# A list scheduler with other costs and finer booking of the weight splits, and local scores that take the two row halves in turn

## What is computed

```python
def first_block(x, p, ...):
    h = rmsnorm(x, norm_mix_g[i]); z = h @ w_in[i]              # 1024 x 5888
    y_a = mixer_a(qa, ka, va, ...) @ w_out_a[i]                 # 8 heads of 128 over 2 key heads
    y_b = mixer_b(qb, kb, vb, rel_bias) @ w_out_b[i]            # 3 dilations x 4 heads of 64, local bands
    x = x + (gate_a * y_a + gate_b * y_b) @ w_out[i]
    x = x + jnp.square(jax.nn.relu(rmsnorm(x, g) @ w_ff1[i])) @ w_ff2[i]
    x = x + jax.nn.sigmoid(rmsnorm(x, g) @ w_ple_gate[i]) * (p[i] @ w_ple[i])

def second_block(x, mem, ...):
    x = x + 0.5 * swiglu(rms_norm(x, ...), ...)
    x = x + hybrid_mixer(...)      # retention, and differential attention: 4 heads, two maps of 64 each
    x = x + memory_attention(...)
    x = x + 0.5 * swiglu(rms_norm(x, ...), ...)
```

## Time and profile before

| | us |
|---|---|
| median of 3 runs | 2070.78 (2067.91 to 2071.4) |
| the profiled execution | 2071.25 |
| its span, first to last instruction | 2069.5 |
| granted TensorE clock, mean | 0.992 |
| TensorE busy | 2037.4 (98%) |
| DVE, ACT, POOL busy | 1122.7, 889.7, 346.8 |

### The profile page before, as it was taken

The page is one execution under the profiler, slowest core; times in us unless marked ns, Lnnn a source line. Parts: engine busy times, 40 slices in busy tenths (PEclk is TensorE's granted clock), DMA queues, the critical chain, the costliest instruction groups (busy, mean ns, idle before and its releaser), DMA issues.

```text
span 2069.5 us, 25244 instructions
## 1 busy us (share of the span) xinstructions
PE 2037.4 (98%) x9854; PEld 1696.8 (82%) x9854; DVE 1122.7 (54%) x1960; ACT 889.7 (43%) x1750; POOL 346.8 (17%) x343
## 2 busy tenths in 40 slices
PE   8999999999999999999999999999999999999997
PEld 6888778888888888878888888788898888888886
DVE  5566775445544344565443435787775664443434
ACT  5344554345433233553332325676655443332324
POOL 3214341032000000342110101232211021110102
PEclk9999999999999999999999999999999999999999
DMA  5121111243333332233232323223242032333222
GB/s 195 62 62 62 51 47 54 86 152 102 104 99 96 98 98 89 86 105 102 93 101 92 102 84 110 77 81 96 86 154 87 29 117 92 101 93 102 92 92 72
DMA packets 61636, 191.54 MB, mean 93 GB/s; under 512 B 6792, under 2 KB 14472, under 8 KB 61516
## 3 DMA queue, kind: packets, MB, share of 16 engines
q1 hardware_dynamic: 61516, 189.93, 28.8%
HBM read 187.69 MB, written 2.21 MB: 92 GB/s over the span
## 4 chain that ended last, share of the span: by engine, by line
PE 92%; DVE 4%; ACT 1%; DMA 1%; issue 0%; SPq 0%; DVEq 0%; ACTq 0%
PE bank L292 91%; PE bank L297 1%; DVE wl L469 0%; DVE tmp L181 0%; DVE work L190 0%; SPq L169 0%; ACT tmp L178 0%; DMA raw<-d_wts 0%; DMA d_tab<-tab_sb 0%; ACT wh L467 0%; ACT rsq L178 0%; DVE x_sb L181 0%; DVE tmp L184 0%; DVE work L181 0%; DVE pd L184 0%
## 5 line engine op out<-in xcount | busy, mean ns | idle before, releaser
L467 ACT ACTIVATE wh<-raw 128x512 fp32r<-128x512 f32 (+1 forms) x700 | 403.3, 609 | 896.9 <-PE bank L292 892.6
L292 PE MATMUL bank<-h_h,wh 128*128 128x512 f32 x1536 | 612.2, 399 | 7.4 <-ACT wh L467 6.4
L292 PE MATMUL bank<-h_l,wh 128*128 128x512 f32 x1536 | 602.9, 393 | 1.0 <-DVE h_l L184 1.0
L292 PE MATMUL bank<-h_h,wl 128*128 128x512 f32 x1536 | 602.4, 392 | 0.0
L469 DVE TENSOR_TENSOR wl<-raw,wh 128x512 fp32r<-128x512 f32 (+1 forms) x630 | 420.6, 693 | 57.1 <-ACT wh L467 35.1
L292 PEld LDWEIGHTS bank<-h_h,wh 128*128 128x128 f32 x1536 | 291.0, 189 | 71.8 <-ACT wh L467 6.4
L292 PEld LDWEIGHTS bank<-h_l,wh 128*128 128x128 f32 x1536 | 291.3, 190 | 63.3 <-DVE h_l L184 3.1
L292 PEld LDWEIGHTS bank<-h_h,wl 128*128 128x128 f32 x1536 | 290.8, 189 | 61.6 <-DVE wl L469 0.3
L469 POOL TENSOR_TENSOR wl<-raw,wh 128x256 fp32r<-128x256 f32 x138 | 109.0, 816 | 363.9 <-ACT wh L467 363.9
L202 POOL TENSOR_TENSOR tmp<-tmp,rstd 128x512 f32<-128x512 f32 x44 | 63.7, 1450 | 469.4 <-ACT tmp L178 469.4
L181 DVE TENSOR_TENSOR tmp<-bank,rstd 128x512 f32<-128x512 f32 x98 | 70.5, 722 | 126.7 <-PE bank L292 126.2
(11 more groups left out here) (476 smaller groups left out, 3352.3 us busy)
## 6 DMA issues: line engine op xcount, KB each, us to landing
raw<-d_wts SPq DMA_DIRECT2D x314, 512.0 KB, 3.5
raw<-d_wts SPq DMA_DIRECT2D x24, 384.0 KB, 3.0
x_sb<-d_xT SPq DMA_DIRECT2D x16, 256.0 KB, 5.2
raw<-d_wts SPq DMA_DIRECT2D x24, 128.0 KB, 2.0
d_yT<-x_sb SPq DMA_DIRECT2D x4, 384.0 KB, 3.0
tab<-d_ali SPq DMA_DIRECT2D x4, 256.0 KB, 4.1
tab<-d_dec SPq DMA_DIRECT2D x4, 256.0 KB, 3.7
mraw<-d_memT SPq DMA_DIRECT2D x8, 128.0 KB, 2.5
```

What stands on the lines that cost most here:

```text
L292: bank.done = pe.add(lambda e: e.matmul(out, lhsT, rhs, start=first, stop=True, skip_group_check=True), n, w, waits)
L467: p.th = [Op(act, lambda e, c=c: e.activation(H[:, c], raw[:, c], FN.Copy), [p.load]) for c in (slice(o, min(o + 512, width)) for o in ran ...
```

## The change

It has two parts that work together. The costs of the scheduler are replaced by others, and the parts of a weight split are booked one by one: after a panel's first two steps 0.61 us each on ACT, after the following two (DVE) or four (POOL) steps 0.69 or 0.8 us each on the engine that makes `wl`. Which engine that is, is now settled two panels ahead (`lows`), not when the panel is taken. Where `place_panels` puts the parts is not changed. And `scores_b` no longer loops over e outside: it takes two banks a piece and issues each matmul for rows 0 to 63 and then for rows 64 to 127.

```diff
     def a_act(out, in_, func, *waits, **kw):
-        cost = 0.1 + 0.00082 * size(in_) + 0.06 * ("bias" in kw) + 0.08 * ("accum_out" in kw)
+        cost = 0.19 + 0.00085 * size(in_) + 0.06 * ("bias" in kw) + 0.19 * ("accum_out" in kw)
...
     def v_tt(out, a, b, op, *waits):
-        return dve.add(lambda e: e.tensor_tensor(out, a, b, op), 0.065 + 0.00105 * size(a), waits)
+        return dve.add(lambda e: e.tensor_tensor(out, a, b, op), 0.14 + 0.00108 * size(a), waits)
...
     def p_mul(out, a, s, *waits):
-        return pool.add(lambda e: e.tensor_scalar(out, a, s, 1.0, ALU.mult, ALU.mult), 0.07 + 0.0012 * size(a), waits)
+        return pool.add(lambda e: e.tensor_scalar(out, a, s, 1.0, ALU.mult, ALU.mult), 0.17 + 0.0016 * size(a), waits)
...
     def b_mm(bank, out, lhsT, rhs, *waits):
         first, w = opened(bank)
-        n = 0.0025 + size(rhs) / 2400
-        n = max(n, 0.055) if lhsT.dtype == F32R else max(4 * n, 0.108)
+        load, n = 0.111 if size(lhsT) == 128 else 0.06, size(rhs) / 2400
+        if lhsT.dtype != F32R:
+            n = max(4 * n + 0.01, 0.112)
+        elif lhsT.shape[0] == 64 and size(lhsT) == 128:
+            n = 0.045 + 0.0002 * size(rhs)
+        else:
+            n = max(n + 0.013, load)
...
     def take(s):
...
-        behind = max(dve.t, pe.t) + 1.2 > max(pool.t, pe.t) + 2.4
-        p.low = low = pool if (behind if i > 3 else i > 0) else dve
+        p.low = low = lows.pop(i) if i in lows else pool if i > 0 else dve
...
     def ran(p):
 
         p.steps.append(marks())
-        if len(p.steps) == 3:
-            parts_here(panels[p.i - 1].done.fin if p.i else 0.0)
+        n, i = len(p.steps) - 2, p.i + 2
+        if n == 0:
+            behind = max(dve.t, pe.t) + 1.39 > max(pool.t, pe.t) + 3.2
+            lows[i] = pool if (behind if i > 3 else i > 0) else dve
+        if n < 2:
+            act.t = max(act.t, panels[p.i - 1].done.fin + 0.13 if p.i else 0.0) + 0.61
+            th_fin[i, n] = act.t
+        elif i in lows or panels[-1].i >= i:
+            low = lows[i] if i in lows else panels[i].low
+            if low is dve and n < 4:
+                dve.t = max(dve.t, th_fin[i, n - 2] + 0.13) + 0.69
+            elif low is pool and n < 6:
+                pool.t = max(pool.t, th_fin[i, (n - 2) // 2] + 0.13) + 0.8
...
     def scores_b(pr, work):
...
-            def scores(b, out, g, lq, rk):
-                q, k = qk[pr][g]
-                b_mm(b, out, q.h[hp, lq], k.h[hp, rk], q.rdy[0], k.rdy[0])
-                b_mm(b, out, q.l[hp, lq], k.h[hp, rk], q.rdy[1])
-                q.free = k.free = [b_mm(b, out, q.h[hp, lq], k.l[hp, rk], k.rdy[1])]
...
+        def scores(bs, outs, g, lq, rk):
+            q, k = qk[pr][g]
+            for x, y, tq, tk in ((q.h, k.h, q.rdy[0], k.rdy[0]), (q.l, k.h, q.rdy[1], None), (q.h, k.l, None, k.rdy[1])):
+                for b, out, hp in zip(bs, outs, heads):
+                    q.free = k.free = [b_mm(b, out, x[hp, lq], y[hp, rk], tq, tk)]
```

More of the change, by code:

```diff
@@ L448, in parts_here @@
         low = (dve if not first_parts else pool) if len(panels) < 3 else panels[-1].low
-        act.t = max(act.t, after) + 1.04
-        low.t = max(low.t, act.t - 0.5) + (2.4 if low is pool else 1.2)
+        act.t = max(act.t, after) + 1.26
+        low.t = max(low.t, act.t - 0.6) + (3.0 if low is pool else 1.39)
     def take(s):
@@ L1001, in scores_b @@
         last = []
+        heads = slice(0, 64), slice(64, 128)
+        was = []
         for e in range(2):
[L1003 removed]
             if p_free[e] is None:
                 yield lambda: p_free[e] is not None
[L1006 to L1014 removed]
@@ new lines, in scores_b @@
+            was.append(p_free[e])
+            p_free[e] = None
+        views = [views_b(e) for e in range(2)]
+        bias0 = [bias_t[0][:, hd * 256:hd * 256 + 256] for hd in (2 * pr, 2 * pr + 1)]
+        def scores(bs, outs, g, lq, rk):
[3 more added lines that the diff above has]
+                    q.free = k.free = [b_mm(b, out, x[hp, lq], y[hp, rk], tq, tk)]
@@ new lines, in exps, with biased @@
+        def exps(e, g, parts):
+            for s, blk, tk in parts:
+                tk = a_act(s, s, FN.Exp, tk, bias=nm[:, e, g, blk:blk + 1], accum_out=ss[:, e, g, blk:blk + 1])
+            last.append(tk)
+        def biased(e, b, g, blks):
+            (g0, g12), w = views[e], was[e]
+            if blks == (1, 2):
+                s = b.ap[:, :].rearrange("p (b k) -> p b k", b=2)
+                t1 = v_tt(g0[:, 1:3, :], s, bias0[e].unsqueeze(1).to_broadcast([128, 2, 256]), ALU.add, b.done, t_toe, w)
+                b.free = [t1]
+                t2 = v_red(nm[:, e, 0, 1:3], g0[:, 1:3, :], ALU.max, t1, negate=True)
+                exps(e, 0, [(g0[:, 1, :], 1, t2), (g0[:, 2, :], 2, t2)])
+            elif blks == (0, 3):
+                p0, p3 = g0[:, 0, 64:256], g0[:, 3, 0:192]
+                t1 = v_tt(p0, b.ap[:, 0:192], bias0[e][:, 64:256], ALU.add, b.done, t_toe, w)
+                t2 = v_tt(p3, b.ap[:, 256:448], bias0[e][:, 0:192], ALU.add, b.done, t_toe, w)
+                b.free = [t2]
+                t3 = v_red(nm[:, e, 0, 0:1], p0, ALU.max, t1, negate=True)
+                t4 = v_red(nm[:, e, 0, 3:4], p3, ALU.max, t2, negate=True)
+                exps(e, 0, [(p0, 0, t3), (p3, 3, t4)])
+            else:
+                bt = bias_t[g][:, (2 * pr + e) * 128:(2 * pr + e) * 128 + 128]
+                s = b.ap[:, :].rearrange("p (c k) -> p c k", c=4)
+                t1 = v_tt(g12[g], s, bt.unsqueeze(1).to_broadcast([128, 4, 128]), ALU.add, b.done, t_toe, w)
+                b.free = [t1]
+                t2 = v_red(nm[:, e, g, :], g12[g], ALU.max, t1, negate=True)
+                exps(e, g, [(g12[g][:, c, :], c, t2) for c in range(4)])
@@ new lines, in scores_b @@
+        for g, blks in ((0, (1, 2)), (0, (0, 3)), (1, None), (2, None)):
+            if not have(*qk[pr][g])():
+                yield have(*qk[pr][g])
+            yield [t.rdy for t in qk[pr][g]]
+            bs = []
+            for e in range(2):
+                bs.append((yield from bank_of(JOB)))
+            act_table(EXP)
+            if g == 0:
+                for n, blk in enumerate(blks):
+                    lo, hi = max(0, 128 * blk - 64), min(S, 128 * blk + 192)
+                    outs = [b.ap[:, 256 * n:256 * n + hi - lo] for b in bs]
+                    scores(bs, outs, 0, slice(128 * blk, 128 * blk + 128), slice(lo, hi))
+            else:
+                for c in range(4):
+                    cs = slice(128 * c, 128 * c + 128)
+                    scores(bs, [b.ap[:, cs] for b in bs], g, cs, cs)
+            for e in range(2):
+                biased(e, bs[e], g, blks)
+            yield
```

60 lines of the change are left out of this document (10 added, 50 removed).

## The result

| | before | changed |
|---|---|---|
| median of 9 runs, us | 2070.78 (2064.98 to 2073.48) | 2075.61 (2073.14 to 2078.7) |
| ratio, 95% interval | | 1.0026 (1.0015 to 1.0037) |
| the profiled execution, its span | 2071.25, 2069.5 | 2078.7, 2076.9 |
| granted clock, mean | 0.992 | 0.991 |

The changed kernel is 0.26% slower, where 1.0% faster was forecast. Its profiled execution lies 3.1 us above its median. In that execution the first wait for a weight panel, at the very start, is 7.8 us, against 6.4 before; the other traces here have 6.1 to 7.2.

A forecast was written before the change was run, and what follows sets the result against it. TensorE, with work for 98% of the span, was taken as the bound; 7.4 + 10.2 + 1.2 + 7.4 - 4.8 = 21.4 us off the profiled 2071.25 gave 2049.9, as a median 2049.4 us, range 2044 to 2055.

The forecast's parts named there:

- part 1: Local scores: matmuls on the two row halves overlap in pairs, saving 72 starts of 0.112 us; 7.4 us gained.
- part 2: Local scores and the stall before them: three half-clock stretches of 6.8 us go, 3.4 us each; 10.2 us gained.
- part 3a: Stall at 44 us: TensorE's wait for the keys `qb011` shrinks from 1.8 to 0.6 us; 1.2 us gained.
- part 3b: Wide attention: 5.7 of 7.2 us of TensorE's waits go, and 1.7 us of half-clock cost; 7.4 us gained.
- part 4: Differential attention: six more of 16 maps have their halves apart, each half paying in full; 4.8 us lost.
- rival 4: Differential attention loses less, 1.6 us in place of 4.8, so 2046.2 us; chance 0.13.
- The rest at nothing.: Everywhere else: nothing gained or lost; 25 more DVE splits lie beside TensorE's panels of 5.4 us each.
- Other waits stay, within the 7.9 us; plus or minus 2.: TensorE's remaining waits stay within the 7.9 us idle in the long full-clock window, plus or minus 2 us.
- Rival 1: Wide attention: new costs shift its chains so others stand still, its 7.4 us gain is lost, 2056.8 us; chance 0.2.
- Rival 5: Wide attention: 16 pairs of blocks each wait 1.29 us behind a DVE split and the clock falls, 2075.1 us; chance 0.04.
- signs of being wrong: Half clock after scores, any `wl` wait, `pa`/`pta_l` waits over 4 us, or over 15 us idle from 240.5 us on.

The follow-up runs named there:

- e1: The kernel before with only the changed `scores_b` (local scores in turn on the two row halves), old costs and booking: 2055.92 us, ratio 0.9934.
- e2: The changed kernel with the old `scores_b` (one half, then the other), new costs and booking: 2086.83 us, ratio 1.0082.
- e8: The changed kernel with old booking throughout, new costs in the first block and old costs in the second: 2048.08 us, ratio 0.9886.
- e3: The changed kernel with the old costs of every instruction, new booking kept: 2057.99 us, ratio 0.9943.
- e4: The changed kernel with the old booking of weight splits in one lump, new costs kept: 2075.04 us, ratio 1.0024.
- e12: e3 with both banks of a map asked for before its first matmul, so its halves stay together: 2057.34 us, ratio 0.9939.
- e5: The changed kernel with new costs for TensorE alone, old ones for ACT, DVE and POOL, new booking: 2049.12 us, ratio 0.9887.
- e14: The changed kernel with queues taken as free 0.05 to 0.10 us before an instruction ends, the old 0.13 delay kept: 2065.54 us, ratio 0.9970.
- e9: The changed kernel with the costs of ACT, DVE and POOL halfway between old and new: 2060.1 us.
- e10: The changed kernel with the costs of ACT, DVE and POOL raised to 1.5 times the step from old to new: 2099.95 us.
- e6: The changed kernel with queues taken as free 0.05 to 0.10 us before an instruction ends, and a delay of 0.05, not 0.13: 2065.33 us, ratio 0.9967.
- e13: e11 with both banks of a map asked for before its first matmul, so its halves stay together: 2046.68 us, ratio 0.9883.
- e11: The changed kernel with old costs and booking in the second block, from one stage later than in e7: 2044.80 us, ratio 0.9878.
- e7: The changed kernel up to the end of the first block, old costs and old booking from there on: 2047.97 us, ratio 0.9882.

## Why the prediction was wrong

**Right: part 1**, the row halves. Four of the twelve pairs of one run of scores in the changed kernel (timeline; "x2" is one on each half):

```profile
36.90 0.38 PE L297 MATMUL bank<-qb001h,qb000h 64*128 64x256 f32 x2
37.13 0.28 PE L297 MATMUL bank<-qb001h,qb000l 64*128 64x256 f32 x2
37.24 0.28 PE L297 MATMUL bank<-qb001l,qb000h 64*128 64x256 f32 x2
...
38.25 0.28 PE L297 MATMUL bank<-qb001l,qb000h 64*128 64x192 f32 x2
```

One pair starts every 0.11 to 0.12 us, 24 matmuls in 1.5. e1 gained 15.1 us, where part 1 and the two stretches of part 2 that went make 14.2.

**Right for two stretches of three: part 2.** Those behind the long runs went with the scores (e1) and came back without them (e2). The one near 46 us stayed, 6.8 us long: 3.4 not gained. The prediction had hung it on **part 3a**, and that term failed: the wait for `qb011` was to shrink from 1.8 to 0.6 and grew to 2.4. That this wait decides the stretch isn't shown: e8 waited 2.5 us there and has no stretch, e2 1.1 us and has one of 3.4. Waits of TensorE after, 12 to 70 us (beside the earlier trace rows), and ACT:

```profile
PE bank L297 <- ACT qb011h L178: 1.5, 1, 1.5
PE bank L297 <- POOL qb011l L202: 0.9, 1, 0.9
```

```profile
42.67 1.15 ACT L471 ACTIVATE wh<-raw 128x512 fp32r<-128x512 f32 x2 [8.41 <-DMA raw<-d_wts]
...
45.70 0.61 ACT L178 ACTIVATE qb011h<-tmp 128x512 fp32r<-128x512 f32 x1
```

I had summed the four exponentials as 0.9 us from DVE's last maximum to 42.8. They take 45.70 - 43.73 = 2.0 (0.49 each), and ahead of them in ACT's queue stand two parts of a weight copy that waited until 42.67 for their DMA. I had looked at what is queued ahead on DVE and not on ACT.

**Right and too small: part 3b.** From matmul 1200 to 2000 the changed kernel gained 10.3 us (e2, with the same costs: 10.3; e1: 0.0), forecast 7.4. Either half of the scheduler's change gives most of it alone: the booking 7.1 (e3), the costs 9.7 (e4). Waits for `pa` and `pta_l` of 7.2 us became 0.3 in all.

**Right: part 4.** A half alone takes what both take together. Timeline of the changed kernel, a half of 384 columns, and what follows it:

```profile
1399.66 0.44 PE L297 MATMUL bank<-qk23h,qk22h 64*128 64x384 f32 x1
1399.94 0.33 PE L297 MATMUL bank<-qk23h,qk22l 64*128 64x384 f32 x1
1400.12 0.33 PE L297 MATMUL bank<-qk23l,qk22h 64*128 64x384 f32 x1
1400.38 0.50 PE L297 MATMUL bank<-std0h,dvh 128*128 128x512 f32 x1
```

0.72 us, forecast 0.71. Likewise 0.89 at 512 columns (0.8), 0.55 at 256 (0.55). Between matmuls 6100 and 6830 the 7.4 us less the 2.6 of mix leave 4.8, the forecast; e12 shows the size from the other side. So rival 4, the smaller loss, fell. The six matmuls of a map of 384 columns that stand three and three took 0.72 to 0.74 us in e12 from the first start to the next instruction's, as three of one half do alone. The Trainium skill, "TensorE: Matmul & The Clock Gate", section "What overlaps and what doesn't", has matmuls keep the program's order, by which three and three would share one pair. The trace doesn't agree, and it doesn't agree either with the sentence under "The chip, the cores and the metric" that each engine works off its queue strictly in order: the row halves on TensorE don't.

**The step that failed: "The rest at nothing." with "Other waits stay, within the 7.9 us; plus or minus 2."** They did not stay: 17.5 - 1.4 = 16.1 us of new waits from 1430 to 1550 us, and there TensorE's 6.10 + 3.40 + 6.45 = 16.0 us of work at half the clock, 8.0 more. Together 24.1, where the table has 7.4 + 16.5 = 23.9 between marks 6830 and 7500, or 26.5 with the mix; the 2.4 between I can't place.

The profiled execution was to take 2049.9 and took 2078.7, 28.8 more. 24.1 of these are this one term. Without it the time would have been inside the range of 2044 to 2055. The small terms nearly cancel: 1.4 more at the start, 4.1 less gained up to the local mixer's end (parts 1, 2 and 3a: 14.7 of 18.8), 2.9 more in the wide attention, 0.3 more behind it; with 26.5 for this stage the sum closes.

I had measured how much cover each chain has on TensorE for the wide attention, found the memory attention's least distance a little shorter, and took that as small; I never counted the cover between stages, 263 matmuls against 107. Both orders could be read.

The scheduler's own clock told it as well: added up over TensorE's bookings, it plans 15.4 us of standing still before and 43.8 after, 24.3 of them in this stage. From TensorE's 6100th to its 7500th booking, which holds the differential attention and most of the memory attention, it plans 0.0 us in e5, 0.9 before, 3.2 in e3, 5.4 in e12, 6.1 in e14, 6.6 in e9, 20.3 in e4, 27.5 in the changed kernel and 38.9 in e10. That is the order of their measured idle times from 1340 us on (0.8, 1.6, 2.3, 5.8, 6.0, 7.8, 14.9, 18.2 and, to 1590 us, 24.1). It fails for e6 (0.0 planned, 5.1 measured) and by less for e13 (1.1 and 3.8). My reason for trusting it in part 3b (better costs, better places) I never turned round to ask what it planned elsewhere.

Rival 1 ("the waits move, they don't go") named the right kind of event, and even the memory attention as a sign of it, but at a price of 7.4, that of part 3b given nothing. Rival 5, the slower one, blamed splits on DVE in the wide attention, which in fact gained; that its 2075.1 lies 0.5 from the measured 2075.6 is luck. That the clock also falls at stalls I had read at 237 us and put on new waits in rival 5 alone. Of the signs of being wrong two came: 20.4 us of idle time from 240.5 us on, against a limit of 15, and a wait for `wl` of 0.3 us, though once and too small to matter.

## What to carry to other kernels

When a scheduler's costs change, count for both orders what stands between a chain's last link and its first use, at every stage border and not only where the old waits were, and print the scheduler's own idle time by stage. The second sorted the orders better than the count did here, but not the one with overlapping costs. Costs that are right for an instruction's length can be wrong as load, and here even the costs nearest to the trace gave a worse order than optimistic ones, so test them by dose and by stage: the same new costs that lose in the memory attention gain in the wide attention, and the fastest kernel (e11) uses them only ahead of the second block's mixers. Keep the part of a change that wins by itself (here `scores_b`, 15 us) apart from a new order of everything.

## What the runs showed of the hardware

- Row halves in turn, in two banks, overlap fully: one pair every 0.11 to 0.12 us at 128 to 256 columns. So do three and three in two banks with nothing between: 0.49, 0.55, 0.72 and 0.89 us for the six matmuls of a map of 128, 256, 384 and 512 columns (e12, to 0.02). Halves with other work between pay in full, 0.48, 0.55, 0.72 and 0.89 us for each three.
- At a granted clock of 0.50 such pairs of 128 columns start every 0.21 to 0.22 us (48.0 to 49.7 us of the changed kernel), against 0.11 at 1.00.
- In a run of 48 matmuls of 64 rows, one half at a time, the granted clock fell to 0.50 some 3.4 to 4.7 us after the run's start, for 6.8 us (twice before, twice in e2); after 24 in pairs at 58.6 and 123.9 us it stayed at 1.00 (e1).
- Waits of 1.8 to 6.6 us of TensorE in the memory attention were followed, or overlapped, by 3.4 to 10.3 us at 0.50 (the changed kernel, e2, e4, e9, e10, e12, e14). In the changed kernel this made a third of the loss there (8.0 of 24.1). But it isn't a fixed price. A wait of 1.7 us at 1485 us of the changed kernel left the clock at 1.00, and so did two of 2.0 to 2.1 us in e6, near 231 and 1462 us, and one of 2.5 near 280 us in e5, while e7 waited 2.2 near 882 us and got 3.4 us at half clock.
